# The even layer's projection in two jobs, with the attention and the pooling in pieces behind the chunks of the second

## What is computed

```python
def even_layer(x, w_in, w_pool, pool_scale, w_out):
    h = x @ w_in                                  # 2048 x 6144
    q, k, v, g_a, u, g_b = jnp.split(h, [1024, 2048, 3072, 4096, 5120], axis=-1)
    o_a = stick_breaking_attention(q, k, v)       # 8 heads of 128
    o_b = multiscale_pool(u, w_pool, pool_scale)  # 4 groups of 256, windows 2, 4, 8, 16
    mixed = concatenate([o_a * silu(g_a), o_b * silu(g_b)])
    return mixed @ w_out                          # 2048 x 2048

def stick_breaking_attention(q, k, v):            # per head and block of 128 queries
    z = (q @ k.T) * scale
    causal = s_idx < t_idx
    log_keep = where(causal, log_sigmoid(-z), 0)
    later = cumsum(log_keep, reverse=True) - log_keep
    weights = where(causal, exp(log_sigmoid(z) + later), 0)
    return weights @ v
```

## Time and profile before

| | |
|---|---|
| median of three runs | 2848.18 us (2842.56 to 2848.41) |
| the profiled execution | 2849.75 us, its span 2848.0 us |
| TensorE (PE) busy | 2546.3 us, 89% |
| weight loads (PEld) | 2112.4 us, 74% |
| VectorE (DVE) busy | 1509.8 us, 53% |
| ScalarE (ACT) busy | 1277.8 us, 45% |
| GpSimd (POOL) busy | 188.2 us, 7% |
| granted TensorE clock, mean | 0.951 |
| chain of waits, by engine | PE 41%, DVE 6%, ACT 3% |
| DMA | 459.27 MB, mean 161 GB/s |

### The profile page before, as it was taken

How to read it: one execution, slowest core, us unless ns; L and a number is a source line. 1 busy time by engine, 2 the same in 40 slices (tenths; PEclk the granted TensorE clock), 3 DMA queues, 4 the chain that set the end, 5 groups by cost and what they waited for, 6 DMA issues and landing times.

```text
span 2848.0 us, 39475 instructions
## 1 busy us (share of the span) xinstructions
PE 2546.3 (89%) x16067; PEld 2112.4 (74%) x16067; DVE 1509.8 (53%) x1914; ACT 1277.8 (45%) x1669; POOL 188.2 (7%) x205
## 2 busy tenths in 40 slices
PE   5999999999699999989997999695999994777785
PEld 4886888878588888878886888584788884666774
DVE  4444554574466666664444444356665543565645
ACT  4434444564455555554444444643354443444332
POOL 1002000000000000000000000000000002243310
PEclk9999999999899999999998999897999996888898
DMA  6655566655355555546554555154466654112052
GB/s 198 194 174 45 178 203 210 205 181 194 130 190 178 180 188 177 177 178 221 192 192 153 193 189 195 45 178 140 163 214 215 221 199 107 49 43 53 14 222 74
DMA packets 231278, 459.27 MB, mean 161 GB/s; under 512 B 9766, under 2 KB 29319, under 8 KB 228844
## 3 DMA queue, kind: packets, MB, share of 16 engines
q1 hardware_dynamic: 221584, 419.99, 44.6%
q0 software_dynamic: 8576, 35.00, 4.7%
q10 hardware_dynamic: 988, 2.41, 0.2%
HBM read 442.64 MB, written 14.71 MB: 161 GB/s over the span
## 4 chain that ended last, share of the span: by engine, by line
PE 41%; DVE 6%; ACT 3%; POOL 2%; issue 2%; DMA 1%; SPq 0%; DVEq 0%; ACTq 0%; POOLq 0%
PE bank L305 12%; PE bank L306 12%; PE bank L307 12%; PE bank L1668 2%; PE bank L1498 1%; DMA raw<-in_od_w_o 1%; PE bank L1724 1%; DVE X L1329 1%; PE bank L1749 1%; DVE d_products L1638 1%; PE bank L1987 0%; DVE d_inverse L1695 0%; PE bank L1520 0%; PE bank L1629 0%; POOL d_t L1572 0%
## 5 line engine op out<-in xcount | busy, mean ns | idle before, releaser
L242 DVE TENSOR_TENSOR w_low<-raw,w_high 128x1024 fp32r<-128x1024 f32 x768 | 930.1, 1219 | 908.0 <-ACT w_high L236 907.3
L236 ACT ACTIVATE w_high<-raw 128x1024 fp32r<-128x1024 f32 x768 | 807.0, 1057 | 988.9 <-PE bank L307 960.1
L305 PE MATMUL bank<-w_high,b_h_high 128*128 128x512 f32 x704 | 277.5, 394 | 8.2 <-DVE w_low L242 5.9
L307 PE MATMUL bank<-w_high,b_h_low 128*128 128x512 f32 x704 | 274.9, 391 | 0.0
L306 PE MATMUL bank<-w_low,b_h_high 128*128 128x512 f32 x704 | 274.7, 390 | 0.0
L305 PE MATMUL bank<-w_high,a_h_high 128*128 128x512 f32 (+1 forms) x640 | 245.8, 384 | 2.1 <-DVE a_bias_rows L754 2.1
L307 PE MATMUL bank<-w_high,a_h_low 128*128 128x512 f32 (+1 forms) x640 | 245.6, 384 | 0.0
L306 PE MATMUL bank<-w_low,a_h_high 128*128 128x512 f32 (+1 forms) x640 | 245.6, 384 | 0.0
L305 PE MATMUL bank<-w_high,d_high 128*128 128x512 f32 x512 | 200.8, 392 | 7.2 <-DVE d_low L2063 7.2
L305 PE MATMUL bank<-w_high,c_x_high 128*128 128x512 f32 x512 | 199.4, 389 | 2.0 <-DVE c_x_low L428 2.0
L307 PE MATMUL bank<-w_high,d_low 128*128 128x512 f32 x512 | 200.2, 391 | 0.0
(11 more groups left out here) (373 smaller groups left out, 3834.0 us busy)
## 6 DMA issues: line engine op xcount, KB each, us to landing
raw<-in_w_up SPq DMA_DIRECT2D x88, 1024.0 KB, 5.1
raw<-in_w_in SPq DMA_DIRECT2D x76, 1024.0 KB, 5.1
raw<-in_ev_w_in SPq DMA_DIRECT2D x48, 1024.0 KB, 5.1
raw<-in_w_down SPq DMA_DIRECT2D x44, 1024.0 KB, 5.0
raw<-in_w_out SPq DMA_DIRECT2D x16, 1024.0 KB, 5.0
raw<-in_ev_w_out SPq DMA_DIRECT2D x16, 1024.0 KB, 5.0
raw<-in_od_w_r SPq DMA_DIRECT2D x16, 1024.0 KB, 5.0
raw<-in_od_w_k SPq DMA_DIRECT2D x16, 1024.0 KB, 5.1
```

The lines of the kernel that those rows point to most:

```text
L236: act.activation(wh[n % 4][:, :, 0:width], raw_half, ACT.Copy).then_inc(sem("w_high_made"), 1)
L242: vec.tensor_tensor(wl[n % 4][:, :, 0:width], raw_half, wh[n % 4][:, :, 0:width].bitcast(F32), ALU.subtract).then_inc(sem("w_low_made"), 1)
L305: pe.matmul(b, xh, wh[n][:, k % 2, 0:width], start=(c == 0 and k == 0), stop=False)
L307: mm = pe.matmul(b, xl, wh[n][:, k % 2, 0:width], start=False, stop=(c == j.chunks - 1 and k == 3))
```

## The change

The projection is cut into two jobs. `even_qkv` is the first six panels (q, k, v) in a loop of three rounds. `even_rest` is the last six panels, written out, so that other work can be put behind each of its 24 chunks. Panels 0 and 1 of it hold the attention's gates, 2 and 3 the pooling's input, 4 and 5 the pooling's gates.

Behind chunks 0 to 3 TensorE turns q and k. Behind chunks 4 to 13 (`STICK_AT = 4`) come the ten steps of the attention. Behind chunks 16 to 19 (`POOL_AT = 16`) come the pooling's sums, behind 18 to 21 its products. ScalarE's and VectorE's parts of a step come one chunk later, behind their splits of that chunk. Silu is applied as the gates' panels are copied out. The pooling's sums use banks 4 to 7, as banks 0 to 3 belong to the stream. The gates of the last two pooling groups and the turns come behind the last chunk; the turns of the attention's half no longer wait for the pooling.

```diff
                                        stop=(c == j.chunks - 1 and k == 3))
                 mm.then_inc(sem("w_used"), 1)
+            if each is not None:
+                each(c)
 
     def evacuate(act, j, p_static, g_end, out, free=None, f=ACT.Copy):
...
-                         None if free is None else lambda: free(p), f)
+                         None if free is None else lambda: free(p), f(p))
                 if post:
                     post(p)
...
@@ -1114,8 +1117,9 @@
     LN = at("c_norm_rows", [128, 2, D], F32, PH + 96)
     if "C" in segments:
         w_ev = kview(a["ev_w_in_2"][0])
-        add_job("even_in", lambda p: (w_ev, 0, (p if isinstance(p, int) else p[0] * 2 + p[1]) * PANEL, PANEL),
-                12, 4, lambda p, c: (ch, cl, 4 * c), 2)
+        add_job("even_qkv", lambda p: (w_ev, 0, (p if isinstance(p, int) else p[0] * 2 + p[1]) * PANEL, PANEL),
+                6, 4, lambda p, c: (ch, cl, 4 * c), 2)
+        add_job("even_rest", lambda p: (w_ev, 0, (6 + p) * PANEL, PANEL), 6, 4, lambda p, c: (ch, cl, 4 * c), 0)
         w_eo = kview(a["ev_w_out_2"][0])
...
 
+    STICK_AT, POOL_AT = 4, 16
+
     def c_pe(pe):
         turn_pe(pe, TC_x, lambda k, t: X[:, t, 128 * k:128 * k + 128], lambda n: c_ready(pe))
-        run_pe(pe, plan["even_in"], turned_ready(pe, TC_x))
-        j = plan["even_in"]
-        turn_pe(pe, TC_f, lambda k, t: PC[:, t, 128 * k:128 * k + 128],
-                lambda n: pe.wait_ge(sem("acc_free"), j.p0 + j.panels + 2))
-        pe.wait_ge(sem("turned_read"), TC_f.first + 8)
-        pe.wait_ge(sem("c_loaded"), 16 * 13)
-        for i in range(8 + 2):
+        run_pe(pe, plan["even_qkv"], turned_ready(pe, TC_x))
+
+        def rows(n):
+            if n == 0:
+                pe.wait_ge(sem("acc_free"), plan["even_qkv"].p0 + 6 + 2)
+            m = TC_f.first + n
+            pe.wait_ge(sem("turned_read"), m - 3)
+            for k in (2 * n, 2 * n + 1):
+                for t in range(2):
+                    tr = pe.transpose(PS[4 + m % 4][:, 256 * (k % 2) + 128 * t:256 * (k % 2) + 128 * t + 128],
+                                      PC[:, t, 128 * k:128 * k + 128], ident[:, :])
+            tr.then_inc(sem("turned"), 1)
+
+        def stick(i):
+            if i == 0:
+                pe.wait_ge(sem("turned_read"), TC_f.first + 8)
+                pe.wait_ge(sem("c_loaded"), 16 * 13)
...
                           ).then_inc(sem("stick_values"), 1)
-        for g in range(4):
-            bank = PS[g]
+
+        def pool_sums(g):
+            bank = PS[4 + g]
+            if g == 0:
+                pe.wait_ge(sem("acc_free"), plan["even_rest"].p0 + 4 + 2)
...
@@ -1195,29 +1215,39 @@
                 mm = pe.matmul(bank[:, 256 * k + 128:256 * k + 256], PC[:, 1, c:c + 128], pools[:, g, 256:384],
                                start=False, stop=True, skip_group_check=True)
             mm.then_inc(sem("pool_sums"), 1)
-        pe.wait_ge(sem("pool_weights_loaded"), 64)
-        for g in range(4):
+
+        def pool_products(g):
             bank = PS[4 + g]
+            if g == 0:
+                pe.wait_ge(sem("pool_weights_loaded"), 64)
             pe.wait_ge(sem("pooled"), g + 1)
-            if g == 0:
-                pe.wait_ge(sem("mixed_made"), 8)
-                pe.wait_ge(sem("stick_exp"), 8)
             for t in range(2):
                 for k in range(2):
                     mm = pe.matmul(bank[:, 256 * t:256 * t + 256], PL[:, 2 * g + k, 128 * t:128 * t + 128],
                                    WP[:, k, g, :], start=(k == 0), stop=(k == 1))
             mm.then_inc(sem("pool_products"), 1)
-        turn_pe(pe, TC_m, lambda k, t: PC[:, t, 128 * k:128 * k + 128], lambda n: pe.wait_ge(sem("mixed_made"), 12))
+
+        def each(c):
+            if c < STICK_AT:
+                rows(2 * c)
+                rows(2 * c + 1)
+            if STICK_AT <= c < STICK_AT + 10:
+                stick(c - STICK_AT)
+            if POOL_AT <= c < POOL_AT + 4:
+                pool_sums(c - POOL_AT)
+            if POOL_AT + 2 <= c < POOL_AT + 6:
+                pool_products(c - POOL_AT - 2)
+        run_pe(pe, plan["even_rest"], each=each)
+        pe.wait_ge(sem("pool_scaled"), 4)
+        turn_pe(pe, TC_m, lambda k, t: PC[:, t, 128 * k:128 * k + 128],
+                lambda n: pe.wait_ge(sem("mixed_made"), 8 if n < 4 else 5 + n))
         run_pe(pe, plan["even_out"], turned_ready(pe, TC_m))
 
     def c_act(act):
         turn_high(act, TC_x, ch)
-        j = plan["even_in"]
-        run_act(act, j, lambda p, t: PC[:, t, bass.ds((p[0] * 2 + p[1]) * PANEL, PANEL)])
-        act.wait_ge(sem("acc_free"), j.p0 + j.panels + 2)
-        act.activation(PC[:, :, 3072:4096], PC[:, :, 3072:4096], ACT.Silu)
-        act.activation(PC[:, :, 5120:6144], PC[:, :, 5120:6144], ACT.Silu).then_inc(sem("silu_made"), 1)
-        for i in range(8 + 1):
+        run_act(act, plan["even_qkv"], lambda p, t: PC[:, t, bass.ds((p[0] * 2 + p[1]) * PANEL, PANEL)])
+
+        def stick(i):
             if i < 8:
                 t = TC[i % 2]
                 act.wait_ge(sem("stick_scores"), i + 1)
...
@@ -1234,22 +1264,31 @@
                 if n >= 2:
                     act.wait_ge(sem("stick_values"), n - 1)
                 act.activation(WT[n % 2][:, :], PS[4 + n % 2][:, 0:384], ACT.Exp).then_inc(sem("stick_exp"), 1)
+
+        def each(c):
+            if STICK_AT < c <= STICK_AT + 9:
+                stick(c - STICK_AT - 1)
+        run_act(act, plan["even_rest"], lambda p, t: PC[:, t, (6 + p) * PANEL:(7 + p) * PANEL], None, None, each,
+                lambda p: ACT.Copy if p in (2, 3) else ACT.Silu)
         turn_high(act, TC_m, ch)
         run_act(act, plan["even_out"], lambda p, t: YC[:, t, PANEL * p:PANEL * p + PANEL])
         norm_act(act, 0)
 
     def c_vec(vec):
         turn_low(vec, TC_x, ch, cl)
-        run_vec(vec, plan["even_in"])
-        for n in range(8):
+        run_vec(vec, plan["even_qkv"])
+        freed = plan["even_rest"].p0 + 2
+
+        def rows(n):
             m = TC_f.first + n
             vec.wait_ge(sem("turned"), m + 1)
             vec.tensor_scalar(FC[:, 2 * n:2 * n + 2, :], PS[4 + m % 4][:, :].rearrange("p (k s) -> p k s", k=2),
                               128 ** -0.5 if n < 4 else 1.0, None, ALU.mult).then_inc(sem("turned_read"), 1)
-        vec.wait_ge(sem("silu_made"), 1)
-        vec.wait_ge(sem("c_loaded"), 16 * 13)
         mask = before[:, :].unsqueeze(1).to_broadcast([128, 2, 128])
-        for i in range(8 + 2):
+
+        def stick(i):
+            if i == 0:
+                vec.wait_ge(sem("c_loaded"), 16 * 13)
             if i < 8:
                 sp = SP[i % 2]
...
@@ -1262,20 +1301,45 @@
             if i >= 2:
                 n = i - 2
                 vec.wait_ge(sem("stick_values"), n + 1)
+                vec.wait_ge(sem("acc_free"), freed + 1 + n // 4)
                 vec.tensor_tensor(PC[:, :, 128 * n:128 * n + 128], PS[6 + n % 2][:, 0:256].rearrange("p (t e) -> p t e", t=2),
                                   PC[:, :, 3072 + 128 * n:3072 + 128 * n + 128], ALU.mult).then_inc(sem("mixed_made"), 1)
-        for g in range(4):
+
+        def pooled(g):
             vec.wait_ge(sem("pool_sums"), g + 1)
-            vec.tensor_copy(PL[:, 2 * g:2 * g + 2, :], PS[g][:, :].rearrange("p (k s) -> p k s", k=2)
+            vec.tensor_copy(PL[:, 2 * g:2 * g + 2, :], PS[4 + g][:, :].rearrange("p (k s) -> p k s", k=2)
                             ).then_inc(sem("pooled"), 1)
-        for g in range(4):
+
+        def pool_out(g):
+            return PC[:, :, 1024 + 256 * g:1024 + 256 * g + 256]
+
+        def scaled(g):
             vec.wait_ge(sem("pool_products"), g + 1)
-            m = PC[:, :, 1024 + 256 * g:1024 + 256 * g + 256]
-            vec.tensor_tensor(m, PS[4 + g][:, :].rearrange("p (t n) -> p t n", t=2),
+            vec.tensor_tensor(pool_out(g), PS[4 + g][:, :].rearrange("p (t n) -> p t n", t=2),
                               prow[:, 256 * g:256 * g + 256].unsqueeze(1).to_broadcast([128, 2, 256]), ALU.mult
                               ).then_inc(sem("pool_scaled"), 1)
+
+        def gated(g):
             vec.wait_ge(sem("pool_scaled"), g + 1)
-            vec.tensor_tensor(m, m, PC[:, :, 5120 + 256 * g:5120 + 256 * g + 256], ALU.mult).then_inc(sem("mixed_made"), 1)
+            vec.wait_ge(sem("acc_free"), freed + 5 + g // 2)
+            vec.tensor_tensor(pool_out(g), pool_out(g), PC[:, :, 5120 + 256 * g:5120 + 256 * g + 256], ALU.mult
+                              ).then_inc(sem("mixed_made"), 1)
+
+        def each(c):
+            if 1 <= c <= 4:
+                rows(2 * c - 2)
+                rows(2 * c - 1)
+            if STICK_AT < c <= STICK_AT + 10:
+                stick(c - STICK_AT - 1)
+            if POOL_AT < c <= POOL_AT + 4:
+                pooled(c - POOL_AT - 1)
+            if POOL_AT + 2 < c <= POOL_AT + 6:
+                scaled(c - POOL_AT - 3)
```

(23 more changed lines are left out.)

## The result

The change made the kernel slower. Its median is 2863.34 us (2854.22 to 2870.14, 16 runs) against 2849.09 (2842.56 to 2856.38, 16 runs). The ratio is 1.0046, with a 95% interval of 1.0033 to 1.0058. In a second set of runs, with a second profile, it was 1.0043 (1.0027 to 1.0059). The forecast was 2857.2, with a range of 2842 to 2866.

What follows compares the result with a forecast made beforehand. The prediction took TensorE's weight stream (89% busy) to bound the kernel, ScalarE's 4.73 us chain the attention. Clock falls 12.8 plus 0.5 for the tail, less 4.3 gained, gave 9.0 us slower: 2848.2 + 9.0 = 2857.2, range 2842 to 2866.

Steps and rivals of the forecast that it cites:

- The wait in the loop: Attention rounds: second split waits for half a chunk before ScalarE's chain; chunk starts 11.46 us apart, 3.29 idle.
- The eight waits: TensorE's waits in eight attention rounds beside the chunks, put at 2.5 to 4.6 us, seven longer than 3 us.
- The sum at full clock: Even layer's stretches without clock falls: 0.5 + 3.0 + 2.3 - 1.5 = 4.3 us gained, 72.1 for 76.45.
- The tail: Last projection product to first output-projection product: 5.84 us against 4.34, a loss of 1.5.
- the turns: Turns of q and k beside chunks: only TensorE's own 4.1 of 7.07 us stays, gain 3.0.
- The clock: Ten attention pieces: 7.5 falls to half clock at 1.7 us each, 12.8, plus 0.5 for the tail.
- those above fell each time: Granted clock after TensorE gaps in the earlier trace: gaps above 3 us always fell, those under 3 us sometimes.
- 24 of the 48 chunks are now written out: Projection: none of the 1,152 products goes away; writing out half the chunks was given no cost.
- The signs: Expected in the changed trace: chunks 11.5 to 14 us apart, pieces' clock 0.8 to 0.9, tail 5.8 us.
- The clock held: Rival: the clock holds or falls in few rounds of the attention pieces; 2843.9 us, 2847.3 with two falls; chance 0.20.
- The hidden case: Rival: attention hides fully beside the chunks, the stage costing only TensorE's work, 44.3 for 76.45 us; 2816 us; chance 0.07.
- The clock never stuck at half: Judges the rival that the clock sticks at half through the ten pieces, rounds of 16.9 us; 2882 us; chance 0.07.

Runs made afterwards that it cites:

- Experiments 1: Changed kernel with ScalarE's and VectorE's attention pieces moved between a chunk's two splits: 2816.53 us, ratio 0.9897 to the kernel before.
- 5: Changed kernel with only ScalarE's attention piece moved between a chunk's two splits, VectorE's behind both: 2827.15 us, ratio 0.9943 to the kernel before.
- 6: Changed kernel with only VectorE's attention piece moved between a chunk's two splits, ScalarE's behind both: 2860.56 us, ratio 1.0050 to the kernel before.
- 4: Changed kernel with Ln replaced by Exp in the attention, dropping two table loads per head (wrong results, timing only): 2830.68 us, ratio 0.9940 to the kernel before.
- Experiment 2: Changed kernel with extra 512-column products on TensorE filling the waits of rounds 1 to 8: 2845.83 us, ratio 0.9999 to the kernel before.
- the cut kernel: Changed kernel without the odd layer, for timing only: 1992.22 us, against 1983.96 for the kernel before cut the same way.
- experiment 3: Kernel before with the last six projection panels written out and nothing put behind their chunks: 2852.1 us, ratio 1.0015 to the kernel before.
- 9 to 12: Four kernels without the odd layer: before 1983.96 us, six panels written out 1985.19, all twelve written out 1984.26, changed 1992.22.

## Why the prediction was right, and where its sizes were off

**The wait in the loop: right.** The step that decided the even layer was the split's wait for half a chunk, ahead of ScalarE's chain. The eight waits were worked out as 3.0, 4.6, 3.3, 4.6, 3.3, 3.3, 3.3 and 2.5 us; the first profile has 3.01, 4.34, 3.36, 4.34, 3.06, 3.06, 3.06 and 2.31. Experiments 1, 5 and 6 show the cause by moving one engine's piece at a time, 4 by shortening the chain.

**The sum at full clock: right, 0.7 off.** 4.3 us gained were worked out. Experiment 2 has the even layer at 334.1 us against 337.7: 3.6 gained. The small misses: the ten pieces took 105.6 us and not 104.0, in part as the first scores waited 0.95 for VectorE's last copies of q and k, so the attention lost 1.0 where 0.5 gained was worked out; the turns cost a little less than their 4.1. The tail took 5.84 us, as worked out.

**The clock: right in kind, too large by 2.7.** The sum had 7.5 falls of 1.7 us, 12.8, and 0.5 for the tail. Six of the eight waits had one (seven in the cut kernel), and the seventh, of 3.06 us, had none, so "those above fell each time", as the prediction has it, is too strong. It rested on two gaps; the trace of before has another, of 7.34 us ending at 30.37, that left the clock at 1.00. The difference between the changed kernel and experiment 2 is 10.6. The records of the falls give nearly the same by themselves: 23.8 us at half clock, 2.0 of them idle, are 10.9 us of work lost. The tail had no fall (1.00). So the even layer lost 10.6 - 3.6 = 7.0, where the sum had 13.3 - 4.3 = 9.0. Both terms are differences to experiment 2, so that they give 7.0 is no check of its own; the 10.9 is one.

**The rest of the loss: missed.** Forecast 9.0, measured 14.2 and 10.8 in two sets. The even layer holds 7.0, so 7.3 and 3.7 are left. The step that was priced at nothing and isn't is "24 of the 48 chunks are now written out": experiment 3 has 4.9 us for it alone, with hardly a change in the even layer. By 9 to 12 nearly nothing is left without the odd layer. That the odd layer makes up the difference is an inference from medians with intervals of some 4 us and from one profile for each set; its mechanism was not found.

So the total came within the range partly by luck. 2.0 us too much in the even layer made up for part of the 4 to 7 that the sum didn't have at all. That the second set's 2858.0 lies by the forecast of 2857.2 is chance.

**The signs.** Chunks started 11.3 to 16.1 us apart where 11.5 to 14 were forecast, the longest being the round with the fall of 6.8 us. The granted clock was 0.90, and the tail took the 5.84 us worked out.

**The rivals.** The clock held through the ten pieces only where the waits were gone, filled or short (at most 1.73 us in experiment 4 and 2.09 in 5). The Trainium skill's rule (TensorE: Matmul & The Clock Gate, HAM oscillation) is that compute much longer than the wait between bursts keeps the clock. As the prediction applied it, it did not hold here: with bursts of 7.1 to 10.7 us in front of them, two to three and a half times as long, waits of 3.01 to 4.34 us lost the clock in six cases of seven. The hidden case was ruled out by the order of two splits and a piece on ScalarE; undoing that order alone brought it about, at 2816.5 against 2816 worked out. The clock never stuck at half; the longest low stretch was 6.8 us.

## What to carry to other kernels

A piece of a serial chain put behind the chunks of a stream was only hidden here where it stood ahead of every wait for the chunk beside it. Behind such a wait, the chunk's own work enters the loop and nothing is gained, even with the engine that runs the chain idle for half the round. Before laying work beside a stream, write down for one round what each engine's queue holds in order, and where each wait ends. Waits of 3 us between dense bursts were mostly paid twice on TensorE, once as idle time (27.5 us here) and once at half clock (10.6).

## What the runs showed of the hardware that was not expected

- Filling waits with 109 useless products of 512 columns (26.0 us of busy time) saved 10.6 us in the stretch, by the clock alone.
- Writing out loop rounds left the loop's own time as it was (261.29 us against 261.00) and moved the median of the whole kernel by 4.9 and 10.8 us, while the kernels cut behind the even layer differed by 1.2 and 0.3, with intervals of some 4 us.
- Two executions of one kernel differed by 7.0 us, all of it ahead of the stage that was looked at, which took 344.68 and 344.73.
- A wait of 2.31 us at the same place left the clock at 1.00 in one execution and was followed by 3.4 us at half clock in another.
